# TensorE waits for its own last tile at fourteen points of its program

## The reference, cut to what matters

```
for i in range(2):
    x = layer_norm(ALPHA * x + mixer_i(x), ...)
    x = layer_norm(ALPHA * x + cross_attention(x, mem, w_q, w_kv, w_o), ...)
    h = x @ ffn_w_in                       # 1024 -> 2 * 2816
    x = layer_norm(ALPHA * x + (silu(h[..., :2816]) * h[..., 2816:]) @ ffn_w_down, ...)
x = x + g1 * (mix(rmsnorm(x)) @ w_out)
h = causal_conv(modulated_rmsnorm(x) @ ffn_up)     # 1024 -> 2 * 2816
x = rmsnorm(x + g2 * ((silu(gate) * value) @ ffn_down))
```

## Time and profile before

| what | value |
|---|---|
| median of 3 runs | 2296.75 us |
| lowest and highest run | 2290.5 and 2320.01 us |
| span of the profiled execution | 2302.4 us |
| TensorE busy (PE), matmuls | 2235.3 us (97%), 18842 |
| TensorE weight loads (PEld) | 2140.7 us (93%), 18846 |
| VectorE, ScalarE, GpSimd busy | 55%, 41%, 13% |
| mean granted TensorE clock | 0.994 |

### The profile page before, as it was taken

The page is one execution under the profiler, slowest core; times in us unless marked ns, Lnnn a source line. Parts: engine busy times, 40 slices in busy tenths (PEclk is TensorE's granted clock), DMA queues, the critical chain, the costliest instruction groups (busy, mean ns, idle before and its releaser), DMA issues.

```text
span 2302.4 us, 47528 instructions
## 1 busy us (share of the span) xinstructions
PE 2235.3 (97%) x18842; PEld 2140.7 (93%) x18846; DVE 1271.0 (55%) x2590; ACT 936.0 (41%) x1547; POOL 298.9 (13%) x318
## 2 busy tenths in 40 slices
PE   7999999999999999989999999999999998999998
PEld 7978999999999996978999999999989898999998
DVE  6477443665553256889463476554165655656513
ACT  4566354332222143478363252222144554444312
POOL 3000300200000052336120110000033002000001
PEclk9999999999999999999999999999999999999999
DMA  6333341255542221200252245553312202333221
GB/s 172 81 94 92 104 143 56 83 140 142 138 137 101 91 66 56 74 2 1 92 164 75 74 110 140 154 144 110 106 49 92 79 20 75 91 104 97 95 106 55
DMA packets 303947, 219.07 MB, mean 95 GB/s; under 512 B 34442, under 2 KB 290384, under 8 KB 303824
## 3 DMA queue, kind: packets, MB, share of 16 engines
q1 hardware_dynamic: 251856, 188.79, 27.4%
q10 hardware_dynamic: 50208, 25.69, 4.3%
q0 software_dynamic: 1760, 2.88, 0.4%
HBM read 207.58 MB, written 2.10 MB: 91 GB/s over the span
## 4 chain that ended last, share of the span: by engine, by line
PE 90%; ACT 4%; DVE 2%; POOL 2%; issue 1%; DMA 0%; DVEq 0%; SPq 0%; POOLq 0%; ACTq 0%
PE bank L714 69%; PE bank L831 5%; PE bank L940 4%; PE bank L910 2%; PE bank L1259 2%; PE bank L1039 1%; PE bank L1210 1%; PE bank L1108 1%; POOL ZS L2562 1%; PE bank L1100 1%; PE bank L1193 1%; ACT SQ L1559 1%; PE bank L1311 1%; ACT BI L1355 1%; POOL ZS L2531 1%
## 5 line engine op out<-in xcount | busy, mean ns | idle before, releaser
L714 PE MATMUL bank<-XH,WH 128*128 128x256 f32 (+1 forms) x3184 | 887.4, 279 | 6.2 <-DVE HF L2245 2.7
L714 PE MATMUL bank<-XH,WL 128*128 128x256 f32 (+1 forms) x3184 | 886.0, 278 | 0.0
L714 PE MATMUL bank<-XL,WH 128*128 128x256 f32 (+1 forms) x3184 | 886.0, 278 | 0.0
L681 DVE TENSOR_TENSOR WL<-RAW,WH 128x2048 fp32r<-128x2048 f32 x160 | 369.4, 2309 | 521.5 <-ACT WH L677 521.5
L714 PEld LDWEIGHTS bank<-XH,WH 128*128 128x128 f32 (+1 forms) x3184 | 599.0, 188 | 7.1 <-issue 4.1
L714 PEld LDWEIGHTS bank<-XH,WL 128*128 128x128 f32 (+1 forms) x3184 | 600.5, 189 | 0.0
L714 PEld LDWEIGHTS bank<-XL,WH 128*128 128x128 f32 (+1 forms) x3184 | 597.4, 188 | 0.2 <-issue 0.2
L677 ACT ACTIVATE WH<-RAW 128x2048 fp32r<-128x2048 f32 x171 | 327.5, 1915 | 584.1 <-PE bank L714 545.6
L714 PE MATMUL bank<-HH,WH 128*128 (+1 forms) x1056 | 293.4, 278 | 0.9 <-DVE HF L2245 0.9
L714 PE MATMUL bank<-HH,WL 128*128 (+1 forms) x1056 | 293.3, 278 | 0.0
L714 PE MATMUL bank<-HL,WH 128*128 (+1 forms) x1056 | 293.2, 278 | 0.0
(11 more groups left out here) (359 smaller groups left out, 3666.6 us busy)
## 6 DMA issues: line engine op xcount, KB each, us to landing
RAW<-in_ffn_w_in SPq DMA_DIRECT2D x88, 512.0 KB, 4.7
MB<-in_mod_w ACTq DMA_DIRECT2D x48, 512.0 KB, 5.0
RAW<-in_ffn_w_down SPq DMA_DIRECT2D x44, 512.0 KB, 4.0
RAW<-in_ffn_up SPq DMA_DIRECT2D x44, 512.0 KB, 4.6
RAW<-in_xa_w_kv SPq DMA_DIRECT2D x32, 512.0 KB, 4.4
RAW<-in_ffn_down SPq DMA_DIRECT2D x22, 512.0 KB, 3.9
RAW<-in_xa_w_q SPq DMA_DIRECT2D x16, 512.0 KB, 4.2
RAW<-in_xa_w_o SPq DMA_DIRECT2D x16, 512.0 KB, 4.0
```

The source lines that it names most:

```text
L681: nc.vector.tensor_tensor(WL[:, par, :], RAW[:, par, :], f32(WH[:, par, :]), ALU.subtract).then_inc(w_split, 1)
L714: mm = nc.tensor.matmul(out_ap[:, cols], l, moving, start=(start and n == 0 and k == 0), stop=(stop and n == len(parts) - 1 and k == len(o ...
```

## The change

A helper `own_tiles(t)` makes TensorE wait until `tile_ready` has reached t, the count that TensorE's own last matmul brings about. It is called at three places in the code: in a stage with halves, between `in_halves` and the loop (executed 5 times); in a stage with a fill, between `first` and `unit(1, 1)` (7 times); and between the memory's keys and values (twice). That is 14 executions. Nothing is removed or moved, and no other engine's program changes.

```
+            def own_tiles(t):
+
+                pe.wait_ge(tile_ready, t)
+
...
                 if halves:
                     in_halves(name, xs, fill, amid)
+                    own_tiles(TILE0[name] + 4)
                     by_pairs(pe, UNITS[name] - 2, lambda i, j: unit(i + 2, j))
...
                     if behind is not None:
                         behind(0, 0)
+                    own_tiles(TILE0[name] + 2)
                     unit(1, 1)
                     by_pairs(pe, UNITS[name] - 2, lambda i, j: unit(i + 2, j))
...
                 unit(0)(3, 1)
+                own_tiles(TILE0[name] + 8)
                 by_pairs(pe, 4, unit(4))
```

## The result

The changed kernel took 2328.99 us, median of 11 runs (2303.74 to 2372.22), where the kernel before took 2305.09 (11 runs beside it, 2289.51 to 2338.49). The ratio is 1.0087, 95% interval 1.0049 to 1.0126: some 20 us slower, where I had forecast 7 us faster. It lies within the 2% that the measurement is asked to tell, but the interval doesn't take in 1, and it lies outside my range (up to 2322).

The account below looks back on a forecast made before the run. TensorE, with matmuls in flight 97% of the span, was taken as the bound. From the profiled 2302.4 us, plus 6.2 for the stops, minus 18.6 for slow matmuls turned fast, came 2290.0 us; range 2280 to 2322.

Parts of the forecast that it names:

- the two paces: TensorE's dense stretches of 256-column matmuls run at 117.6 or 113.2 ns each, at clock 1.00, with nothing between.
- what a slow matmul costs: Each slow matmul on TensorE takes 4.4 ns more; 4224 slow ones behind new stops turned fast give back 18.6 us.
- the cost of the stops: At 14 points on TensorE: nine at 0.32 us, five with loop set-up at 0.67, together 6.2 us, bounds 4.5 and 8.5.
- No other engine hides the stop: At all 14 stops the wait costs its full time, TensorE being the bound.
- the 13.1 us of the first feed-forward: Part of the 18.6 us gain: its slow loop and down projection turn fast behind the new stop.
- I take the first: Choice among bounds for the pace behind stops: all stretches there go fast, giving 18.6 us; forecast chance 0.50.
- a wait carried by the load favours the fast pace: Stops whose wait sits on the weight load itself favour 113.2 ns, from the stops at 2172.16 and 1950.69.
- the profiled execution as the starting point: The sum starts from the profiled 2302.4 us, its span 5.65 us above the median of the runs.
- The second: Rival: each stop draws the pace again, three fast in four; 2301 us, single executions 2290 to 2331; chance 0.20.
- The first: Rival: stretches behind stops followed by loop set-up, in the ffn_in and values' loops, start slow; 2331 us; chance 0.15.
- The third: Rival: a stop leaves TensorE's pace alone, so there are costs only; 2309 us; chance 0.10.
- the fourth: Rival: TensorE's granted clock falls after each of 14 stops, 14 x 2 us; 2337 us; chance 0.02.

Follow-up runs that it names:

- e4: Kernel before, with a stop ahead of every tile in the loops of ffn_in0 (own wait last) and ffn_in1 (own wait first); 2389.1 us, one execution.
- e5: Kernel before, with one stop a unit in ffn_in1 and four fp32 transposes a unit in ffn_in0; 2312.22 us, one execution.
- e11: Kernel before, with each ffn_in loop cut into five loops of four units, each behind a stop; its time is given under e15.
- e15: The kernel of e11, timed against the kernel before; 2327.87 against 2300.79, ratio 1.0131.
- e14: The kernel of e1 again, on a chip whose kernel before took 2300.79; 2320.73 us, ratio 1.0098.
- e8: Kernel before, with stops ahead of the ffn_in loops, first two units written out, own wait behind that for a free tile; 2301.58 us, ratio 1.0006.
- e13: The changed kernel again, all 14 stops, beside the kernel before; 2323.71 against 2300.79, ratio 1.0106.
- e10: Kernel before, with stops ahead of the ffn_in loops, first two units written out, own wait ahead of that for a free tile; 2312.21 against 2313.37, 0.9991.
- e1: Kernel before, with only the three stops ahead of the ffn_in loops; 2321.65 against 2311.7, ratio 1.0049.
- e6: Kernel before, with 16 fp32 transposes, one tile, then a stop ahead of each feed-forward's loop; 2321.2 against 2297.73, ratio 1.0102.
- e12: The changed kernel once more, all 14 stops, for a second trace; 2299.97 us, one execution.
- e9: Kernel before, with four transposes ahead of units 2, 3 and 4 of each feed-forward and the fill stops except mla_o's; 2301.45 against 2313.37, 0.9954.
- e17: The kernel of e9 again, on another chip; 2300.0 against 2300.93, ratio 0.9993.
- e18: The kernel of e17 without its six stops, only the groups of four transposes; 2298.85 us, ratio 0.9994 to the kernel before.

## Why the prediction was wrong

- **Right: the bound, the two paces, and what a slow matmul costs.** They are in every trace at clock 1.00, and they explain most of the spread of the traced executions: 4.45 ns by the count of slow matmuls leaves 9 us between the spans of eight of them, and 3.5 us once the stops are taken off.
- **Right but for one: the cost of the stops.** 0.33 us for 0.32 (nine), 0.61 for 0.67 (four), 5.4 for 6.2 in sum. "No other engine hides the stop" failed at ffn_in2: VectorE held TensorE there for 2.95 us before and after, and the stop cost nothing.
- **Right, but chance: the 13.1 us of the first feed-forward.** It had a slow opening in the trace of before and in that of after, and there the stop did turn it fast, as in 7 of 7 such cases.
- **Wrong: "I take the first" — that all stretches behind stops go fast.** A stop isn't a reset to the fast pace. Behind a fast opening of a feed-forward it gave the slow pace in 5 of 7. Often it swaps the pace, but that depends on the form and the place: 60 of 60 in e4's first loop and e5, 32 of 47 singly, 21 of 40 in e4's second loop, and none of 13 behind the fast loops of four units in e11. I had argued from what ran fast behind the stops of the earlier trace rows and not from what ran *ahead* of them. That a wait carried by the load favours the fast pace fell as well: single ones turned slow to fast 17 times and fast to slow 15 times. I also counted only what could turn from slow to fast: the second feed-forward, fast in the one trace I had, stood in the sum with nothing to lose, and so would the first wherever it opens fast. The stake is 13.2 us each; e14 shows both lost, 26.5 us. (The third feed-forward's loop was slow behind its wait for VectorE in e4, which has no stop there, in e8 and in e13; what a hidden stop does to it isn't shown.)
- **Wrong: the profiled execution as the starting point.** I saw that the runs could differ by two or three stretches of 13 us, and still subtracted from the pattern of one execution. Its slow first feed-forward isn't in every execution: the fastest four of the twelve runs beside e14, 2289.96 to 2292.95, leave no room for one (by an estimate from the slow matmuls: the fewest outside the feed-forwards in any trace here are some 2300 in e10, and 2275.2 us with these and one slow feed-forward of 3136, 24.2 us, comes to a span of 2299.4). How common it is changes with the session and its chip: the kernel before had medians of 2297.73, 2300.79, 2300.93, 2311.7 and 2313.37 beside the experiments, while e14 and e1 stood at 2320.73 and 2321.65, so the size of a loss here depends also on how the kernel before fared. That most timed executions open fast, are turned slow by the stops and lose 20 us by it is an inference; timed executions have no trace. For it: e14's 2321.65 with a trace and its median 2320.73, and the loss with the three loop stops alone (1.0049 in e1, 1.0098 in e14) is about that with all fourteen (1.0087, 1.0106 in e13).
- **The rivals.** The second, a draw at each start, was nearest in mechanism, though with its three fast in four it gave 2301, and the outcomes don't look drawn: behind a slow opening of a feed-forward 7 of 7, behind a fast one 2 of 7 went fast, and e4's and e5's loops repeat themselves. The first gave 2331, nearest to the measured 2328.99, but for a reason that fell: loops don't start slow by their form (15 of 15 fast in e11), and stops without a loop lost too (e6). The third fell with the pace changes at the stops, the fourth with clock 1.00 in every window shown, right behind the stops too.
- **The rule weighed.** By the Trainium skill, "TensorE: Matmul & The Clock Gate", section "Back-to-back issue gap", an isolated matmul of one width has one gap, 109.2 ns as I estimate for 256 columns; the same section says that in a stream of weight loads and matmuls, as here, both set the spacing, and gives one figure a width for that too (about 81 ns at 128 columns, 131 at 512). With one pace a width a stop would only cost. The traces stand against it as before: 113.2 and 117.6 ns, for the same instructions, at the same clock.

**What stays open.** What decides a single stop. The gap differs by 3 to 4 ns between a stop behind the fast and one behind the slow pace (333 and 337, which is the slower pace itself). Over all stops that a load carries behind the fast pace, those of 333 ns turned the pace slow 35 times of 35, those of 334 in 12 of 16 (slow at xa_o0 in e13, fast at the queries in e12), and the two of 335 left it fast. So the outcome goes with the length of the gap to about 1 ns, the step of the trace. Why isn't shown; a phase finer than that would fit, and it was not tried. Nor have I a trace of the changed kernel at its median: of its three profiled executions two were faster than it, and e13's has the slow piece of attention in it. The piece costs some 38 us, by the spans of one kernel in e1 and e14 (2359.6 - 2319.8, less 1.4 us for e1's 307 more slow matmuls). Without it e13's 2363.03 would be some 2325, near its kernel's median of 2323.71. That is an estimate; in that execution the second feed-forward is the one turned slow by its stop, and the third's loop is slow behind its wait for VectorE.

## What to carry to other kernels

Divide length by count in every dense stretch, in several traces of the same kernel, before a pace is credited or blamed: here 3000 matmuls in a row run 4% slower or not, by what happened at their head, and one execution's pattern is no baseline. A wait of an engine for its own last instruction isn't a way to reset it: it costs 0.3 to 0.6 us, and it can turn a good stretch bad as well as the reverse, so every stretch behind it belongs in the sum, first of all those that run well now. Where the engine waits longer for another at the same place, the new wait costs nothing. And a profiled execution says what is possible, not what is typical: compare its own time with the median before building on it, and a kernel only with runs of the other beside it.

## What the runs showed of the hardware that I had not expected

- **Two stable paces of TensorE at full clock, which a stop can exchange.** For load and matmul pairs of 256 columns 113.2 and 117.6 ns, each kept for up to some 3000 pairs through loop turns, other weights' slots and bursts of DMA; strict alternation over 40 and 20 stops in a row in e4 and e5, and a pattern that repeats every twelve stops in e4's second loop.
- **The cost of a wait for oneself depends on what carries it:** from last start to restart 0.33 us on a weight load, 0.41 to 0.43 where an instruction ahead of the load carries it (e4's second loop, e6, e8), 0.62 with a loop's set-up behind it. The restart itself takes 0.22 to the second matmul in all.
- **A few transposes often end at the fast pace:** after two swaps, 18 groups of four in e5 left it fast, and all loops of e9, e17 and e18 were fast behind three groups; yet behind the 16 of dsa_o it was slow in every trace, behind those of mla_o in all but e13's, and behind the 16 of e6 fast twice and slow once.
